# Two transformer blocks on one core: the order of the first scan, a later slot for the key norms, and a final norm on tokens in partitions

## What is computed

```python
        u_lat = modulate(rmsnorm(h_lat, norm_mix_g[l]), m_lat[0], m_lat[1])
        ...
    oa_ctx, state_a = run_a(a_ctx, zeros_a) 
    ob_ctx, state_b = run_b(b_ctx, zeros_b)
        ...
        h_lat = h_lat + m_lat[2] * y_lat
        h_lat = h_lat + m_lat[5] * hier_moe(...)
    return rmsnorm(h_lat, final_norm_g)
```

## Time and profile before

| what | value |
|---|---|
| median of three runs | 2603.41 us (2602.01 to 2605.66) |
| the profiled execution | 2594.85 us |
| its span, first to last instruction | 2593.1 us |
| busy: PE, DVE, ACT, POOL | 95%, 55%, 46%, 12% of the span |
| mean granted clock of TensorE | 0.977 of 2.4 GHz |
| read from memory, written | 391.59 MB, 1.05 MB |

### The profile page before, as it was taken

One profiled execution on the slowest core, in us unless ns is written; L12 is line 12 of the kernel. 1 busy time (PEld: TensorE's weight loads), 2 busy tenths in 40 slices (PEclk: granted clock), 3 DMA queues, 4 the chain that ended last, 5 costly groups with the idle time before them and its releaser, 6 DMA issues.

```text
span 2593.1 us, 52413 instructions
## 1 busy us (share of the span) xinstructions
PE 2456.9 (95%) x23231; PEld 2123.9 (82%) x23231; DVE 1417.3 (55%) x2210; ACT 1188.9 (46%) x1712; POOL 306.5 (12%) x425
## 2 busy tenths in 40 slices
PE   6999999999999999999999999999888879999998
PEld 5999887799999998878899984786467778878886
DVE  4654545366646645442666556454345551279885
ACT  4434456444444444474444345331254432277773
POOL 0100000031101100000311000461133331000000
PEclk8999999999999999999999999999989999999999
DMA  6754522356656654323566521101200003479993
GB/s 215 247 200 156 189 91 98 114 195 202 228 171 223 224 187 165 116 98 114 171 203 227 181 68 64 67 3 38 98 3 4 4 6 131 131 256 364 367 368 122
DMA packets 268884, 396.07 MB, mean 153 GB/s; under 512 B 9320, under 2 KB 172829, under 8 KB 268525
## 3 DMA queue, kind: packets, MB, share of 16 engines
q1 hardware_dynamic: 266921, 389.25, 44.0%
q0 software_dynamic: 1120, 2.17, 0.3%
q10 hardware_dynamic: 612, 1.24, 0.1%
HBM read 391.59 MB, written 1.05 MB: 151 GB/s over the span
## 4 chain that ended last, share of the span: by engine, by line
PE 75%; DVE 7%; DMA 6%; issue 5%; ACT 4%; POOL 2%; SPq 0%; ACTq 0%; POOLq 0%; DVEq 0%
PE ps L282 74%; DMA RB<-in_moe_w_up 5%; DVE gwl L431 2%; POOL H L1415 2%; ACT gwh L422 1%; POOL AR L2535 0%; ACT wh L422 0%; PE ps L1093 0%; DVE wl L431 0%; ACT AR L2752 0%; ACT AR L2744 0%; DVE AR L1677 0%; DMA RB<-in_ffn_w_gu 0%; DVE AT L1178 0%; DVE AR L1900 0%
## 5 line engine op out<-in xcount | busy, mean ns | idle before, releaser
L431 DVE TENSOR_TENSOR wl<-RB,wh 128x2048 fp32r<-128x2048 f32 (+4 forms) x188 | 412.3, 2195 | 293.7 <-ACT wh L422 293.1
L282 PE MATMUL ps<-H,RB 128*128 128x256 f32 (+1 forms) x1712 | 457.4, 425 | 1.1 <-ACT H L1515 1.1
L422 ACT ACTIVATE wh<-RB 128x2048 fp32r<-128x2048 f32 (+4 forms) x188 | 342.1, 1823 | 235.9 <-PE ps L282 203.9
L282 PEld LDWEIGHTS ps<-H,RB 128*128 128x128 f32 x1712 | 327.1, 194 | 115.1 <-issue 76.4
L282 PE MATMUL ps<-xhf,wl 128*128 128x256 f32 x1408 | 404.3, 287 | 14.0 <-DVE xlf L651 9.2
L282 PE MATMUL ps<-xlf,wh 128*128 128x256 f32 x1408 | 400.9, 285 | 0.0
L282 PE MATMUL ps<-xhf,wh 128*128 128x256 f32 x1408 | 400.7, 285 | 0.0
L282 PE MATMUL ps<-AR 64*64 64x64 f32 (+4 forms) x8296 | 268.3, 238 | 45.6 <-issue 18.1
L282 PEld LDWEIGHTS ps<-AR 64*64 64x64 f32 (+2 forms) x8296 | 235.5, 144 | 78.4 <-issue 50.4
L282 PEld LDWEIGHTS ps<-xhf,wl 128*128 128x128 f32 x1408 | 272.9, 194 | 24.9 <-DVE wl L431 15.6
L282 PEld LDWEIGHTS ps<-xlf,wh 128*128 128x128 f32 x1408 | 272.9, 194 | 0.1
(11 more groups left out here) (428 smaller groups left out, 4142.1 us busy)
## 6 DMA issues: line engine op xcount, KB each, us to landing
RB<-in_ffn_w_gu SPq DMA_DIRECT2D x88, 1024.0 KB, 7.7
RB<-in_w_in SPq DMA_DIRECT2D x25, 2048.0 KB, 7.7
RB<-in_ffn_w_down SPq DMA_DIRECT2D x16, 2048.0 KB, 7.8
RB<-in_w_gate SPq DMA_DIRECT2D x16, 2048.0 KB, 8.8
RB<-in_moe_w_gate SPq DMA_DIRECT2D x32, 1024.0 KB, 7.6
RB<-in_moe_w_up SPq DMA_DIRECT2D x32, 1024.0 KB, 10.2
RB<-in_moe_w_down SPq DMA_DIRECT2D x32, 1024.0 KB, 8.3
RB<-in_ada_w SPq DMA_DIRECT2D x12, 2048.0 KB, 9.8
```

Of the source, the lines that this page charges most:

```text
L282: return M.matmul(o, lhsT, rhs, start=start, stop=stop, skip_group_check=True)
L422: S.activation(self.pair(h)[0], of(slot_of(*key)), ACT.Copy).then_inc(*did("high", *mark))
L431: V.tensor_tensor(lo, of(slot_of(*key)), hi.bitcast(F32), ALU.subtract).then_inc(*did("low", *mark))
```

## The change

It has three parts.

**The scan's order.** `base_a` of a pair comes first; the odd unit's `out` and `state` (unit n - 3) now follow it, ahead of `base_b`, and no longer stand before level 5 of their own pair. `form` of unit n + 3 moves ahead of `mid` of level 5. The decayed queries leave `form_dve` and get a slot of their own, `decay`, after level 1, for both units of a pair from unit 4 on. `out` and `state` of unit 5 stand at the end of the list.

**The key norms** move by one slot: 6 to 9 in place of 5 to 8.

**The end.** `keep` writes the output in rounded parts: ACT the high part into `xh`, DVE the remainder into `xl`. `BACK` is rounded, and `spread` uses 64 rounded products; each waits only for its own half of its own group. `finish` is gone; a class `Finish` is woven into the branch: as soon as a block of `XT` is there, ACT scales it with the norm's gain into `HA` and squares it into `HB`, PE transposes the scaled block and sums the squares with two columns of ones as the moving operand, so that the sums have tokens on partitions. Root and reciprocal act on 128x2. The last ACT and DVE pieces multiply by the token's reciprocal while they copy from PSUM, and four stores of 256 KB follow. An activation of Sqrt on constants stands ahead, so that the table is loaded early. Both branches get it.

```diff
@@ -1689,11 +1689,14 @@
             for n in range(0, 8, 2):
-                order += [("base_a", n, 0), ("base_b", n, 0), ("scale", n, 0)]
+                order += [("base_a", n, 0)]
+                order += [("out", n - 3, 0), ("state", n - 3, 0)] if n > 2 else []
+                order += [("base_b", n, 0), ("scale", n, 0)]
                 order += [("apply", n - 2, 0)] if n else [("z", 1, 0)]
...
                 order += [("more", n, 1)]
+                order += [("decay", n, 0), ("decay", n + 1, 0)] if n > 3 else []
                 order += [("new", n - 2, 0)] if n else []
@@ -1706,11 +1709,9 @@
                 order += [("more", n, 4)]
-                order += [("out", n - 1, 0), ("state", n - 1, 0)] if n else []
-                order += [("mid", n, 5)]
                 order += [("form", n + 3, 0)] if n < 6 else []
-                order += [("more", n, 5)]
-            return order + [("apply", 6, 0), ("apply", 7, 0)]
+                order += [("mid", n, 5), ("more", n, 5)]
+            return order + [("out", 5, 0), ("state", 5, 0), ("apply", 6, 0), ("apply", 7, 0)]
@@ -2105,11 +2106,14 @@
                         *did("qk_dec", u.n))
-                    for e in range(2):
-                        qe = u.QE.rearrange("p h (e c) n -> p e h c n", e=2)[:, e]
-                        ins = V.tensor_tensor(qe, qe, QT.rearrange("p (c h) n -> p h c n", h=2)[:, :, :, chunk(u, e)],
-                                              ALU.mult)
-                    ins.then_inc(*did("q_dec", u.n))
+            def decay_dve(u):
+                DV.wait_ge(*at("exp_g", u.n))
+                for e in range(2):
+                    qe = u.QE.rearrange("p h (e c) n -> p e h c n", e=2)[:, e]
+                    ins = V.tensor_tensor(qe, qe, QT.rearrange("p (c h) n -> p h c n", h=2)[:, :, :, chunk(u, e)],
+                                          ALU.mult)
+                ins.then_inc(*did("q_dec", u.n))
@@ -2418,8 +2424,8 @@
                         ins.then_inc(*did("shift", n))
-                    if 5 <= n < 9:
-                        kj = n - 5
+                    if 6 <= n < 10:
+                        kj = n - 6
                         ps = bank(("sum", f"kk{kj}"), ("root", f"kk{kj}"))
@@ -3338,15 +3343,14 @@
-                finish(area, "d")
...
-            S1, CW, BACK = area(4096, 4, T), area(5120, 4, 8), area(0, 4, T)
-            Y = H.rearrange("p a n -> p (a n)").rearrange("p (g n) -> p g n", g=4)
+            S1, CW, BACK = area(4096, 4, T), area(5120, 4, 8), sb("gbk", STAGE, [4, T], F32R)
+            end = Finish(area, "g")
@@ -3397,12 +3401,18 @@
                 PE.wait_ge(*at("back", 2))
-                PE.wait_ge(*at("y_kept", 3, 1))
                 for c in range(KD):
-                    ps = bank(("spread", c), ("moe_in", c), among=work)
+                    ps = bank(("spread", c), ("moe_in", c), among=(0, 1, 2))
                     for g in range(4):
-                        ins = mm(ps[:, 0:T], Y[:, g, 128 * c:128 * c + 128], BACK[:, g, :], g == 0, g == 3)
+                        PE.wait_ge(*at("y_kept", g, c // 4))
+                        for part in (xl, xh):
+                            ins = mm(ps[:, 0:T], part[:, c, 128 * g:128 * g + 128], BACK[:, g, :], g == 0 and part is xl,
+                                     g == 3 and part is xh)
                     ins.then_inc(*did("spread", c))
+                    if c:
+                        end.pe(c - 1)
+                end.pe(KD - 1)
@@ -3424,6 +3434,12 @@
                         ws.high(downs[e] + 3)
+                    elif what == "keep":
+                        AC.wait_ge(*at("ed", 8 * e + 7))
+                        for o in range(2):
+                            S.activation(xh[:, 4 * o:4 * o + 4, 128 * e:128 * e + 128], ps_of("y", e, o).rearrange(
+                                "p (c n) -> p c n", c=4), ACT.Copy).then_inc(*did("yk_high", e, o))
+                end.act()
@@ -3445,18 +3461,21 @@
                         g = e
-                        DV.wait_ge(*at("ed", 8 * g + 7))
                         for o in range(2):
-                            V.tensor_copy(Y[:, g, 512 * o:512 * o + 512], ps_of("y", g, o)).then_inc(*did("y_kept", g, o))
+                            own = (slice(None), slice(4 * o, 4 * o + 4), slice(128 * g, 128 * g + 128))
+                            DV.wait_ge(*at("yk_high", g, o))
+                            V.tensor_tensor(xl[own], ps_of("y", g, o).rearrange("p (c n) -> p c n", c=4),
+                                            xh[own].bitcast(F32), ALU.subtract).then_inc(*did("y_kept", g, o))
                 for c in range(KD):
...
                                            in1=XT[:, c, :], op0=ALU.mult, op1=ALU.add).then_inc(*did("moe_in", c))
+                end.dve()
...
             vector()
-            everyone(("moe_in", 7))
+            end.store()
@@ -3573,52 +3596,77 @@
                                            op1=ALU.add).then_inc(*did("moe_in", c))
+                end.dve()
...
             vector()
-            everyone(("moe_in", 7))
-        def finish(area, tag):
-            st = "end_" + tag
-            YO = area(0, 2, DM)
-            def tensor():
-                sum_pe(st, HA, both_squares(st))
-                for t in range(2):
-                    for c in (0, 4):
-                        for x in range(4):
-                            PE.wait_ge(*at("normed", st, c + x))
-                        turn(("turned", st, t, c), [("out_v" if c else "out_a", st, t)],
-                             [HA[:, c + x, 128 * t:128 * t + 128] for x in range(4)])
-            def scalar():
-                squares_act(st, XT, HA)
-                root_act(st, T, 1.0 / DM, EPS[:, 0:1], RST)
-                for t in range(2):
-                    AC.wait_ge(*at("turned", st, t, 0))
-                    S.activation(YO[:, t, 0:512], ps_of("turned", st, t, 0), ACT.Copy).then_inc(*did("out_a", st, t))
-            def vector():
-                squares_dve(st, XT, HA)
-                root_dve(st, RST)
+            end.store()
+        class Finish:
+            def __init__(self, area, tag):
+                self.st, self.YO, self.ms, self.rs = "end_" + tag, area(0, 2, DM), RST[:, 0:2], RST[:, 2:4]
+            def pe(self, c):
+                st = self.st
+                if c == 0:
+                    self.ps = bank(("sum", st), ("root", st), among=(3,))
+                PE.wait_ge(*at("normed", st, c))
+                for t in LAT:
+                    if c % 4 == 0:
+                        bank(("turned", st, t, c), ("out_v" if t else "out_a", st, t, c), among=(4, 5, 6, 7))
+                    ps = ps_of("turned", st, t, c // 4 * 4)
+                    ins = M.transpose(ps[:, 128 * (c % 4):128 * (c % 4) + 128], HA[:, c, 128 * t:128 * t + 128], ident)
+                    if c % 4 == 3:
+                        ins.then_inc(*did("turned", st, t, c - 3))
+                PE.wait_ge(*at("squared", st, c))
+                for t in LAT:
+                    ins = mm(self.ps[:, 2 * t:2 * t + 2], HB[:, c, 128 * t:128 * t + 128], ones[:, 0:2], c + t == 0,
+                             c == KD - 1)
+                if c == KD - 1:
+                    ins.then_inc(*did("sum", st))
+            def act(self):
+                st = self.st
+                S.activation(self.ms, EPS, ACT.Sqrt).then_inc(*did("root", st, 0))
+                for c in range(KD):
+                    AC.wait_ge(*at("moe_in", c))
+                    S.activation(HA[:, c, :], XT[:, c, :], ACT.Identity, scale=vec(R_FG + c)).then_inc(
+                        *did("normed", st, c))
+                    S.activation(HB[:, c, :], XT[:, c, :], ACT.Square).then_inc(*did("squared", st, c))
+                AC.wait_ge(*at("sum", st))
+                AC.wait_ge(*at("root", st, 0))
+                S.activation(self.ms, ps_of("sum", st)[:, 0:4].rearrange("p (t n) -> p t n", t=2)[:, :, 0], ACT.Sqrt,
+                             bias=EPS[:, 0:1], scale=1.0 / DM).then_inc(*did("root", st))
+                AC.wait_ge(*at("rstd", st))
+                for c in (0, 4):
+                    AC.wait_ge(*at("turned", st, 0, c))
+                    S.activation(self.YO[:, 0, 128 * c:128 * c + 512], ps_of("turned", st, 0, c), ACT.Identity,
+                                 scale=self.rs[:, 0:1]).then_inc(*did("out_a", st, 0, c))
+            def dve(self):
+                st = self.st
+                DV.wait_ge(*at("root", st))
+                V.reciprocal(self.rs, self.ms).then_inc(*did("rstd", st))
                 DV.wait_ge(*at("rstd", st))
-                for c in range(KD):
-                    V.scalar_tensor_tensor(out=HA[:, c, :], in0=XT[:, c, :], scalar=vec(R_FG + c), in1=RST, op0=ALU.mult,
-                                           op1=ALU.mult).then_inc(*did("normed", st, c))
-                for t in range(2):
-                    DV.wait_ge(*at("turned", st, t, 4))
```

(21 more changed lines are left out.)

17 lines of the change are left out of this document (11 added, 6 removed).

## The result

| what | before | after |
|---|---|---|
| median on the same chip | 2604.44 us (2602.01 to 2605.66, 4 runs) | 2577.57 us (2572.08 to 2583.00, 4 runs) |
| ratio, after to before | | 0.9898, 95% interval 0.9874 to 0.9921 |
| the profiled execution, its span | 2594.85, 2593.1 us | 2579.31, 2577.6 us |
| mean granted clock | 0.977 | 0.980 |

Faster, by 27 us or 1.0% (21 to 33 us by the interval). The forecast was 2587.9, with a range of 2580.0 to 2596.5: the direction was right, the size too small, and the result lies 2.4 us under the range.

A forecast was written before the change was run, and what follows sets the result against it. The prediction took TensorE (PE), with 75% of the chain, to bound the kernel. Its terms, -11.7 + 0.3 - 4.4 + 0.3 = -15.5 us, from the median 2603.41 gave 2587.9 us, with a range of 2580.0 to 2596.5.

The forecast's parts named there:

- What bounds the kernel: Whole kernel: PE carries 75% of the chain; edits pay only at its waits, its own work, or the end.
- The end, -11.7: Final spread and norm: rounded products woven with the norm, PE setting the pace, save 11.7 us (bounds 9.5 and 13).
- Rival D: The new end runs at 1.2 GHz, costing 8 to 12 us more: 2598 us; chance 0.06.
- The kept outputs, +0.3: Expert outputs, groups 0 to 2: splitting into rounded parts costs 0.1 us per group, 0.3 in all; upper bound 2.
- The shift stage, -4.4: Shift stage: 5.1 us of PE waits on key squares go, 0.7 us comes back late in slot 9.
- Rival C: Shift stage keeps a wait: VectorE's lateness is handed on, only 1.5 of 5.1 us return; 2591 us, chance 0.05.
- The level-5 mask: First scan: GpSimd's level-5 mask falls behind the next decay masks, PE waits; pair two's base products come 1.35 us later.
- rival B: First scan: stands before level 5 drop the clock, up to 2 us more at each of three boundaries; 2593, chance 0.18.
- The first scan, +0.3: First scan: -0.55, -0.55, +1.35, +0.2 and -0.3 sum to +0.15 us, rounded up to 0.3; the least certain term.
- rival A: First scan: shorter stands may keep the clock up, 5 us back at most; 2583 us, chance 0.19.
- Pair four, -0.3: First scan's last pair: no next masks, last level no longer behind a state update; 0.3 us gain allowed.
- The base: Differences taken from the profiled execution (2594.85 us, 8.6 under the median) were applied to the median of 2603.41.

The follow-up runs named there:

- e1_end: The kernel before with only the change's new end; 2585.81 us, ratio 0.9951 to the kernel before.
- e3_spread: The kernel before with the change's keep, BACK and rounded spread, the old finish behind it; 2591.49 us, ratio 0.9968.
- e1_before: The kernel before, run again unchanged; 2596.89 us, ratio 0.9996.
- e2_form: The whole change with form of unit n + 3 put back between mid and more of level 5; 2571.57 us, ratio 0.9899 to the kernel before.
- e3_stand: e3_both with the base copy of units 4 and 6 done seven times instead of once; 2585.04 us, ratio 0.9953 to the kernel before.
- e2_state: The kernel before with only the odd unit's out and state moved behind the next base copies in pairs two to four; 2591.93 us, ratio 0.9979.
- e1_scan: The kernel before with only the change's scan order and decay slot; 2592.50 us, ratio 0.9972.
- e2_last: The whole change with unit 5's out and state put back before level 5 of the last pair; 2570.33 us, ratio 0.9891 to the kernel before.
- e3_table: e3_both with the Sqrt activation on constants moved right behind the last expert's Silu; 2570.69 us, ratio 0.9892 to the kernel before.
- e3_both: The whole change with the edits of e2_last and e2_form together; 2569.28 us, ratio 0.9887 to the kernel before.

## Why the prediction was right in direction and too small

- **What bounds the kernel**: right. PE, its stands and the end; every difference that an edit made lies there.
- **The end, -11.7**: right. -11.16 in the traces, -12.7 (7.8 to 17.7) alone. The block's 1.62 us came out at 1.63; the issue and landing of the stores were undersized by 1 us. PE's stand ahead of the first scaled block was put at 0.7 us; the forecast's own times, 2562.2 and 2562.6, give 0.4, and the trace 0.22. Rival D (the end at 1.2 GHz) did not happen: the clock was 1.00 from 2555 to 2572.
- **The kept outputs, +0.3**: +0.26 in the trace of after, -0.04 in e1_end and -0.36 in e3_spread (against e1_before): nothing that can be told.
- **The shift stage, -4.4**: right. -5.5 in the traces (all 5.1 of the waits, 0.3 instead of 0.7 given back, less waiting in smaller pieces), -4.4 alone. Rival C is out.
- **The level-5 mask**: the mechanism was right and well sized where it stood alone (pair one +1.14 for +1.35; stands of 2.2 us as forecast). e2_form puts it at 5.6 us for pairs one to three in the traces (3.4 of it half-rate time), 5.0 in the medians. So rival B came about in part: 3.4 us at half rate lie at pair two's stand of 2.2 us in three of five traces, behind pair three's in none.
- **The first scan, +0.3: the step that failed**, by 7.6 us. It priced each boundary by its instructions, 0.55 us earlier each, and left all else of pairs two and three as it was, the half-rate time included. In pair three that time was a consequence of the very stand that the change shortens (e3_stand, e2_state): 10.2 us at half rate, 5.1 us. The prediction had this as rival A, with a chance of 0.19 and "5 us back at most", which is that pair alone. The way to price it was in the earlier trace rows: 10.3 us at 1.2 GHz in pair three against 1.00 in pair four. It held against A that pair two fell to 0.88 after a stand of 1.08 us only. That objection stands: the change does not shorten this stand (0.95 us, with 1.4 us more ahead of it), and yet the 6.8 us behind it, worth 3.4, are gone in all five traces with its order. Why is open. Together pairs two and three had 17 us at half rate, 8.5 us.
- **Pair four, -0.3**: wrong sign. The prediction saw that its last level no longer stands behind a state update, and not who waits for that update when it goes to the end of the list: +3.2 us in the trace, 3.0 by the traces of the repair.
- **The base**: "I take differences from this execution and apply them to the median" hid the rest of the miss in the scan. The table's clock of 1.00 in pair four was one of two draws. The execution stood 8.6 us under the median, and the prediction said so, but asked of no row what could be missing from it. By the three traces of five, 0.6 x 6.85 = 4.1 us of the median is, as an estimate, half-rate time behind the fourth boundary, which none of the five traces with the new order has. The four rows of the scan in the table add to -3.5; with -4.1 that makes -7.6, against the -7.3 of e1_scan.

With -7.3 for the scan the sum gives -23.1, and 2580.3: just inside the range, 2.7 us from the result. That the two traced executions differ by exactly the forecast -15.5 is luck: the scan's rows lie 3.6 us under what was worked out for them, the start 1.2 and the shift stage 1.1, and untouched code ahead of the experts gives 5.5 back.

## What to carry to other kernels

Price a stand of TensorE as its length and the half-rate time that stands behind it in the table by stretch; when a change shortens the stand, that time belongs to the sum, with a chance of its own, since here the same stand in the same code had it in some executions and not in others. Before a profile is taken as the base, ask how far it lies from the median, and read the clock of like stretches against each other: where one of two equal stands is followed by half rate, the other may be in some executions, as here. When a step is moved to the end of a list, look for the first reader behind it, and walk every engine's list (here GpSimd's masks): a slot that helps one engine moved work in front of another's.

## What the runs showed that was not expected

- Of stands in this scan, those of 3.3 us were followed by 10.2 us at half rate in both cases; those of 2.9 us by 10.2 us at the third boundary in all six traces that have one there, and at the fourth by 13.7 us in three of five; those of 2.2 us in front of level 5 by 3.4 us in pair two of three traces (the change each time), by none in e1_scan, e2_last and everywhere in pair three; those of 1.39 us at the scan's end by 3.4 us (the change's three traces), 6.8 us (e2_form) or none (e1_scan); those of 0.85 and 1.5 us by none.
- Pair two's stand of 1.08 us stands outside any order by length. In twelve traces the code up to it and behind it, as far as level 3 of the pair, is the same, and 6.8 us at half rate follow in eight: in all seven with `form`, decays and pair one as before, and in one (e3_table) of the five with the repaired order. e3_table and e3_both, with the same scan, take 26.91 and 24.03 us there. What decides it, no run shows.
- Over the runs of the sets the mean clock tells the scan's part by itself: 0.9754 for before in the first set, 0.9785 with the new order alone, 0.9753 and 0.9758 with the key norms or the end alone. (0.9785 - 0.9754) x 2595 = 8 us less lost to the clock, about what e1_scan gained. e1_before, with no change at all, has 0.9757.
- Executions of one kernel differ by up to 18 us (before: 2587.15 to 2605.19), and code that no kernel changes, from the shift stage's end to the first expert, takes 432 to 441 us between kernels. Its half-rate stretches fall differently each time, but that is not all: the traces of before and after both have 41 us at half rate there, and differ by 5.5 us. A difference of 5 us between two traces is not yet one of the kernels.
